# Where the softmax's normalisation is done: from a scaled identity on TensorE to a multiply on GpSimd, with the score scale moved into the exponential

## The chip, the cores and the metric

The kernel runs on one NeuronCore of a Trainium2 chip. The metric is the device time of one execution in microseconds (us). Engines are named as in the profile: PE is TensorE's matmul (PEld its weight load), DVE is VectorE, ACT ScalarE, POOL (Pool) GpSimd, SP SyncE.

## The reference

One encoder block over 512 tokens of width 2048, in fp32. A normed and modulated input is projected once; the projection feeds two groups of eight attention heads. Then come an output projection and an MLP. What matters here is the attention, where all heads look at all 512 tokens:

```
def block(i):                                   # group A: 8 query heads, 2 key heads, width 128
    s = einsum("bkgqd,bksd->bkgqs", qb, k) * (1 / sqrt(128))
    p = softmax(s, axis=-1)
    return einsum("bkgqs,bksd->bkgqd", p, v)

def block(i):                                   # group B: 8 heads, own keys, plus a shared rotary key of 64
    s = (einsum("bhqd,bhsd->bhqs", qn, k_nope)
         + einsum("bhqr,bsr->bhqs", qp, k_pe)) * (1 / sqrt(192))
    p = softmax(s, axis=-1)
    return einsum("bhqs,bhsd->bhqd", p, v)

o = concatenate([rms_norm(o_a, g_out_a), rms_norm(o_b, g_out_b)])     # over each group's 1024 columns
```

The rms_norm of the attention's outputs needs, for each token, the sum of squares over the heads of its group.

## The kernel before

Every matmul operand is split in a high and a low part of type fp32r, so that a product is three matmuls (high x high, high x low, low x high). ACT makes the high part, a copy rounded to fp32r, and DVE the low part, the difference (names ending in _hi and _lo). fp32 matmuls without that split are used only where the operand must not be rounded, as in the turning of the probabilities.

The stages follow each other: projection (blocks of 512 columns), latent keys and values, attention, output projection, MLP. Each engine runs its own program in order; semaphores tie them together. In the attention stage, the 16 heads run one after the other: head H is 0 to 7 for group A and 8 to 15 for group B. The tokens that ask are cut in four blocks t of 128.

For head H and block t:
- PE, `scores`: three matmuls of 512 columns (six in group B, where the rotary part is added) into bank[t].
- DVE, `row_max`: the negated maximum of each row into `top`. The queries had been multiplied by 1/sqrt(128) or 1/sqrt(192) when ACT copied them out of PSUM (`copy_out`, `turned_copy`).
- ACT, `exp`: prob = exp(score + top), with the row sums in `total` (a second record, the read of the accumulator).
- DVE, `invert`: the reciprocal of the sum, then scale_p = identity x reciprocal (128x128).
- PE, `turn_probs` (a "turn"): four fp32 matmuls, stationary operand a 128x128 piece of prob and moving operand scale_p. They transpose the piece and normalise it in one go. Blocks 0 and 3 share bank 4, so turn 3 waits until turned_lo(0) has read it.
- ACT, `turned_hi`, and DVE, `turned_lo`: the high and low part of the turned probabilities (pt_hi, pt_lo).
- PE, `attend`: when all four low parts are there, the product with the values, twelve matmuls into bank 6 (lines 1918 to 1920).
- ACT, `head_out` and `head_squares`: copy the product of head H-1 out, and square it into sq. Pool, `add_squares`, adds sq to sq_sum. head_squares(H) waits until Pool has added the square before it, since sq is one buffer.

The heads overlap by a written order. While head H's probabilities are turned, the scores of head H+1 are made: PE runs turn 0, turn 1, scores 0, turn 2, scores 1, turn 3, scores 2, scores 3, product. DVE runs turned_lo(0), row_max(0), turned_lo(1), turned_lo(2), row_max(1), invert(0), turned_lo(3), row_max(2), invert(1), row_max(3), invert(2), the low part of the next query (q_lo), invert(3); row_max and invert are head H+1's. ACT runs turned_hi(0), turned_hi(1), head_squares, turned_hi(2), exp(0), turned_hi(3), exp(1), exp(2), the high part of the next query, exp(3). head_out stands ahead of turned_hi(0) in group A. In group B there come besides: on ACT the high part of the values (v_hi) at the head's start, and after exp(3) those of the rotary query (qr_hi) and the key (k_hi); on DVE their low parts v_lo, at the head's start, and qr_lo and k_lo, at its end. The next head's scores 0 wait for k_lo. The next query's high part waits for all scores of the head before it.

Pool does nothing else in this stage. Ahead of it, it sets sq_sum to zero; behind it, it issues the loads of the residual once the sums of squares have been reduced. In the first head, DVE also has a part of the gate's modulation to do (`modulate_out`, tile ga_acc), between q_lo and the first turned_lo.

Of the kernel before, what the change touches and what calls it, by code (L numbers as in the profile page):

```python
# [26 lines left out]
P = 128  # L27
T = 512
NT = T // P
# [6 lines left out]
HEADS = 8  # L36
# [111 lines left out]
def build(nc, a, out, x1_dram, y_dram):  # L148
    with ExitStack() as ctx:
# [36 lines left out]
        rstd = small("rstd", [NT, 4])  # L186
        top = small("top", [NT])
        total = small("total", [NT])
        rtotal = small("rtotal", [NT])
# [11 lines left out]
        prob = sb("prob", 52, [NT, T])  # L201
        scale_p = sb("scale_p", 178, [NT, P])
        kg_hi, kg_lo = sb("kg_hi", 60, [2, T], F32R), sb("kg_lo", 64, [2, T], F32R)
# [110 lines left out]

        s_done, nb_ready, exp_done, rt_ready = sems("s_done nb_ready exp_done rt_ready")
        p_turned, pt_hi_done, pt_done, pv_done, o_done = sems("p_turned pt_hi_done pt_done pv_done o_done")
# [309 lines left out]
        def _(act):  # L626
# [61 lines left out]
            def copy_out(b):  # L688

                s = sets[b % 2]  # L690
                if b == 0:
                    for t in range(NT):
                        nc.scalar.activation(tok[:, t, :], s[t][:], ACT.Square, accum_out=stat[:, t, 0:1]).then_inc(c_sq, 1)
                elif b == 1:
                    for t in range(NT):
                        nc.scalar.activation(tok[:, t, 0:2 * P], s[t][:, 0:2 * P], ACT.Copy)
                        nc.scalar.activation(v_gqa[:, t, :, :].rearrange("p g e -> p (g e)"), s[t][:, 2 * P:4 * P], ACT.Copy).then_inc(copied, 1)
                elif b <= 4:
                    for t in range(NT):
                        nc.scalar.activation(tok[:, t, :], s[t][:], ACT.Copy).then_inc(copied, 1)  # L700
                elif b <= 6:
                    for n in range(4):
                        nc.scalar.activation(q_o[:, HEADS + 4 * (b - 5) + n, :], s[n][:], ACT.Copy, scale=SCALE_B).then_inc(copied, 1)
                elif b <= 8:
                    for n in range(4):
                        nc.scalar.activation(k_nope[:, 4 * (b - 7) + n, :], s[n][:], ACT.Copy).then_inc(copied, 1)
                else:
                    for t in range(NT):
                        dst = v_lat[:, t, 4 * (b - 9):4 * (b - 9) + 4, :].rearrange("p h e -> p (h e)")
                        nc.scalar.activation(dst, s[t][:], ACT.Copy).then_inc(copied, 1)  # L710

            def turned_copy(b):

                for n in range(TURNS[b]):
                    act.wait_ge(turned, TURNS_SUM[b] + n + 1)
                    src = sets[b % 2][n][:]
                    if b == 0:
                        k = 3 * KD + 2 * HEADS + n
                        nc.scalar.activation(ckv[:, n, :], src, ACT.Copy, scale=gains[:, k:k + 1]).then_inc(turned_out, 1)
                    elif b == 1:  # L720
                        nc.scalar.activation(k_gqa[:, n, :], src, ACT.Copy).then_inc(turned_out, 1)
                    elif b <= 3:
                        nc.scalar.activation(q_o[:, 4 * (b - 2) + n, :], src, ACT.Copy, scale=SCALE_A).then_inc(turned_out, 1)
                    else:
                        nc.scalar.activation(q_rot[:, n, :], src, ACT.Copy, scale=SCALE_B).then_inc(turned_out, 1)

# [86 lines left out]

            def exp(t, H):
                act.wait_ge(nb_ready, H * 4 + (t + 1))
                nc.scalar.activation(prob[:, t, :], bank[t][:], ACT.Exp, bias=top[:, t:t + 1], accum_out=total[:, t:t + 1]).then_inc(exp_done, 1)

# [13 lines left out]
            def attend(cur, nxt, after, first=False):  # L831
# [15 lines left out]
                if nxt:  # L847
                    exp(0, nxt[2])
                turned_hi(3, H)
                if nxt:  # L850
                    exp(1, nxt[2])
                    exp(2, nxt[2])
                if after:
                    stage_q(*after)
                if nxt:
                    exp(NT - 1, nxt[2])
                if after and after[0]:
# [4 lines left out]
            for t in range(NT):  # L862
                exp(t, 0)
            stage_q(*A(1))
# [189 lines left out]
        def _(dve):  # L1054
# [280 lines left out]

            def row_max(t, H):

                dve.wait_ge(s_done, H * 4 + (t + 1))
                nc.vector.reduce_max(top[:, t:t + 1], bank[t][:], AX.X, negate=True).then_inc(nb_ready, 1)

            def invert(t, H):

                dve.wait_ge(exp_done, H * 4 + (t + 1))
                own.step(nc.vector.reciprocal(rtotal[:, t:t + 1], total[:, t:t + 1]))
                ts(scale_p[:, t, :], ident[:], rtotal[:, t:t + 1], None, ALU.mult).then_inc(rt_ready, 1)

# [5 lines left out]
            def attend(cur, nxt, after):  # L1352
# [4 lines left out]
                if nxt:  # L1357
                    row_max(0, nxt[2])
                turned_lo(1, H)
                turned_lo(2, H)  # L1360
                if nxt:
                    row_max(1, nxt[2])
                    invert(0, nxt[2])
                turned_lo(3, H)
                if nxt:
                    for t in (2, 3):
                        row_max(t, nxt[2])
                        invert(t - 1, nxt[2])
# [12 lines left out]
            for t in range(NT):  # L1381
                row_max(t, 0)
                if t:
                    invert(t - 1, 0)
# [335 lines left out]
        def _(pe):  # L1720
# [170 lines left out]
            def turn_probs(t, H):  # L1891
                pe.wait_ge(rt_ready, H * 4 + (t + 1))

                behind = {0: 0, 1: -2, 2: -1, 3: 1}[t]
                if not isinstance(H, int):
                    pe.wait_ge(pt_done, H * 4 + behind)
                elif H * 4 + behind > 0:
                    pe.wait_ge(pt_done, H * 4 + behind)
                for c in range(NT):
                    ins = mm(bank[TURN_BANK[t]][:, c * P:(c + 1) * P], prob[:, t, c * P:(c + 1) * P], scale_p[:, t, :], start=True, stop=True)  # L1900
                ins.then_inc(p_turned, 1)
# [203 lines left out]
        def _(pool):  # L2105
# [8 lines left out]
            own.step(nc.gpsimd.memset(kr_lo[0:64, 1, :].bitcast(F32), 0.0))  # L2114

            def add_squares(H, grp):

                pool.wait_ge(o_done, H + 1)
                if not (isinstance(H, int) and H == 0):
                    pool.wait_ge(sq_ready, H)  # L2120
                tt(sq_sum[:, grp, :], sq_sum[:, grp, :], sq[:], ALU.add).then_inc(sq_ready, 1)

            pool.wait_ge(mod_reduced, NB + 3)
            own.step(nc.gpsimd.memset(sq_sum[:], 0.0))
            add_squares(0, 0)
            with pool.Fori(1, HEADS) as h:
                add_squares(h, 0)
            with pool.Fori(HEADS, 2 * HEADS - 1) as h:
                add_squares(h, 1)

# [80 lines left out]
```

## Time and profile before

| | |
|---|---|
| median of 3 runs | 2241.33 us (2238.19 to 2241.94) |
| profiled execution, its own time | 2241.33 us |
| its span, first to last instruction | 2239.7 us |
| busy: PE, DVE, ACT, POOL | 94%, 66%, 37%, 3% |
| mean granted TensorE clock | 0.978 of full |
| attention stage in the span | about 510 to 687 us |

A line of instructions has the start in us from the span's start, the duration in us, the engine, the line of the kernel, the operation, the tile written, the tiles read, and their shapes; "x16" says that sixteen records in a row were put together, and in square brackets stands how long the engine had been idle before it and who ended that. A fp32 matmul leaves two records, other matmuls one. PE's ends are modelled.

### The profile page before, as it was taken

The numbers are of one execution on the slowest core, as the hardware profiler recorded it, in microseconds if no ns is written. First come the engines' busy times: TensorE is split into PE (matmuls) and PEld (weight loads), VectorE is DVE, ScalarE is ACT, GpSimd is POOL, SyncE is SP. The second block draws the span as 40 slices with busy tenths as digits, with TensorE's granted clock in tenths as the row PEclk, the third lists the DMA queues.
The fourth block names the chain that finished last, engine by engine and source line by source line (L and its number), as shares of the span: only waits on it lengthen the run. The fifth ranks groups of instructions, "written<-read, shape, count | busy, mean of one in ns | idle before, by whom it ended". The sixth has DMA issues, their size and how long they took to land.

```text
span 2239.7 us, 27119 instructions
## 1 busy us (share of the span) xinstructions
PE 2115.9 (94%) x9652; PEld 1757.2 (78%) x9652; DVE 1477.7 (66%) x1754; ACT 821.4 (37%) x1103; POOL 74.9 (3%) x85
## 2 busy tenths in 40 slices
PE   2479999998999998999999999999999999999998
PEld 2368888887888887888888888888878888888886
DVE  5755687468775666554454455444688888889866
ACT  3233322246774235332332233233333333333322
POOL 0000000001110000000000000002100000000000
PEclk9679999999999999999999999999999999999999
DMA  8865666681004653476566556656774564456451
GB/s 298 292 227 175 205 169 194 191 259 57 1 0 157 212 194 137 143 247 215 179 211 232 184 184 231 212 179 235 292 275 152 221 233 175 172 225 257 157 186 76
DMA packets 199609, 427.76 MB, mean 191 GB/s; under 512 B 29908, under 2 KB 55160, under 8 KB 190712
## 3 DMA queue, kind: packets, MB, share of 16 engines
q1 hardware_dynamic: 180824, 349.89, 47.0%
q0 software_dynamic: 16704, 67.11, 8.4%
q10 hardware_dynamic: 2016, 9.90, 1.1%
q8 instruction: 40, 0.66, 0.1%
q14 instruction: 25, 0.20, 0.0%
HBM read 359.75 MB, written 67.11 MB: 191 GB/s over the span
## 4 chain that ended last, share of the span: by engine, by line
PE 85%; DVE 6%; DMA 4%; issue 2%; ACT 2%; SPq 0%; DVEq 0%; ACTq 0%; POOLq 0%
PE bank L1742 12%; PE bank L1743 12%; PE bank L1744 12%; PE bank L2035 6%; PE bank L2037 6%; PE bank L2036 6%; PE bank L1730 6%; PE bank L1731 6%; PE bank L1732 6%; DMA raw<-in_w_ada 2%; PE bank L1900 2%; DVE start_acc L1114 1%; PE bank L2082 1%; PE bank L2083 1%; PE bank L2084 1%
## 5 line engine op out<-in xcount | busy, mean ns | idle before, releaser
L1062 DVE TENSOR_TENSOR lo<-raw,hi 128x1024 fp32r<-128x1024 f32 x232 | 278.1, 1203 | 474.0 <-ACT hi L633 473.6
L633 ACT ACTIVATE hi<-raw 128x1024 fp32r<-128x1024 f32 x232 | 239.6, 1038 | 741.3 <-PE bank L1744 482.9
L1742 PE MATMUL bank<-h_hi,hi 128*128 128x512 f32 x1152 | 449.7, 390 | 3.5 <-DVE h_lo L1493 3.5
L1744 PE MATMUL bank<-h_hi,lo 128*128 128x512 f32 x1152 | 448.8, 390 | 0.0
L1743 PE MATMUL bank<-h_lo,hi 128*128 128x512 f32 x1152 | 448.7, 390 | 0.0
L2035 PE MATMUL bank<-hi,y_use 128*128 128x512 f32 x784 | 306.5, 391 | 7.7 <-DVE acc L1637 3.8
L2037 PE MATMUL bank<-hi,y_use 128*128 128x512 f32 x784 | 305.1, 389 | 0.0
L2036 PE MATMUL bank<-lo,y_use 128*128 128x512 f32 x784 | 305.1, 389 | 0.0
L1005 ACT ACTIVATE hi<-w 128x1024 fp32r<-128x1024 f32 x168 | 178.4, 1062 | 294.8 <-PE bank L2037 217.6
L1742 PEld LDWEIGHTS bank<-h_hi,hi 128*128 128x128 f32 x1152 | 216.6, 188 | 48.8 <-DVE h_lo L1493 3.7
L1743 PEld LDWEIGHTS bank<-h_lo,hi 128*128 128x128 f32 x1152 | 216.7, 188 | 45.1 <-issue 0.2
L1744 PEld LDWEIGHTS bank<-h_hi,lo 128*128 128x128 f32 x1152 | 216.6, 188 | 45.1
L1561 DVE TENSOR_TENSOR lo<-w,hi 128x1024 fp32r<-128x1024 f32 x168 | 204.4, 1221 | 40.8 <-ACT hi L1005 39.4
L2035 PEld LDWEIGHTS bank<-hi,y_use 128*128 128x128 f32 x784 | 147.1, 188 | 44.1 <-issue 13.9
L2037 PEld LDWEIGHTS bank<-hi,y_use 128*128 128x128 f32 x784 | 147.1, 188 | 30.7
L2036 PEld LDWEIGHTS bank<-lo,y_use 128*128 128x128 f32 x784 | 147.2, 188 | 30.1
L1730 PE MATMUL bank<-hi,h_hi 128*128 128x512 f32 x320 | 128.6, 402 | 0.7 <-issue 0.7
L1731 PE MATMUL bank<-lo,h_hi 128*128 128x512 f32 x320 | 127.0, 397 | 0.0
L1732 PE MATMUL bank<-hi,h_lo 128*128 128x512 f32 x320 | 126.6, 396 | 0.0
L1637 DVE TENSOR_TENSOR acc<-bank,acc 128x1024 f32<-128x1024 f32 x84 | 102.3, 1218 | 0.0
L1730 PE MATMUL bank<-hi,o_hi 128*128 128x512 f32 x224 | 89.2, 398 | 0.4 <-issue 0.4
L1114 DVE SCALAR_TENSOR_TENSOR start_acc<-raw,silu_c,start_acc 128x1024 f32<-128x1024 f32 x56 | 71.0, 1281 | 25.5 <-DMA raw<-in_w_ada 25.4
(274 smaller groups left out, 2871.0 us busy)
## 6 DMA issues: line engine op xcount, KB each, us to landing
raw<-in_w_ada SPq DMA_DIRECT2D x192, 512.0 KB, 4.7
raw<-in_w_mlp_in SPq DMA_DIRECT2D x128, 512.0 KB, 3.9
w<-in_w_mlp_out SPq DMA_DIRECT2D x128, 512.0 KB, 5.3
y_dram<-y_out POOLq DMA_DIRECT2D x32, 1792.0 KB, 8.3
y_use<-y_dram SPq DMA_DIRECT2D x53, 1024.0 KB, 8.8
raw<-in_w_in SPq DMA_DIRECT2D x32, 512.0 KB, 4.4
raw<-in_w_out SPq DMA_DIRECT2D x32, 512.0 KB, 4.6
raw<-in_w_in SPq DMA_DIRECT2D x48, 256.0 KB, 3.4
```

What stands on the lines that cost most here:

```text
L633: ins = nc.scalar.activation(dst, src, ACT.Copy)
L1062: ins = tt(dst, src, high.bitcast(F32), ALU.subtract)
L1561: tt(lo[w.slot()][:], weight(np, i, h)[:], hi[w.slot()][:].bitcast(F32), ALU.subtract).then_inc(dn_lo, 1)
L1730: mm(acc[t][:], xh, hi[s][:, q, :], start=first and q == 0, stop=False)
L1731: mm(acc[t][:], xh, lo[s][:, q, :], start=False, stop=False)
L1732: ins = mm(acc[t][:], xl, hi[s][:, q, :], start=False, stop=last and q == QROWS - 1)
L1742: mm(acc[n][:], wh, act_hi[:, k, :], start=first and q == 0, stop=False)
L1743: mm(acc[n][:], wh, act_lo[:, k, :], start=False, stop=False)
L1744: ins = mm(acc[n][:], wl, act_hi[:, k, :], start=False, stop=last and q == QROWS - 1)
L2035: mm(bank[b + m][:], yh, hi[s][:, q, :], start=j == 0, stop=False)
L2036: mm(bank[b + m][:], yh, lo[s][:, q, :], start=False, stop=False)
L2037: ins = mm(bank[b + m][:], yl, hi[s][:, q, :], start=False, stop=j == PAIRS - 1)
```

## The change

The normalisation goes from PE to Pool. scale_p and its build fall away; `invert` only makes the reciprocal. A new function on Pool, `normalise`, multiplies prob in place by the reciprocal of its row, one 128x512 multiply for each block, and a new semaphore p_ready lets PE turn the block, now by a transpose with the plain identity. On Pool the order becomes normalise(0), normalise(1), and then, for each following head, normalise(h+1) and add_squares(h-1); the last add follows the loop.

The score scale goes from the queries' copies into `exp`. The queries stay unscaled; row_max makes the plain maximum, and a second DVE instruction multiplies it by minus the scale into nbias.

```
-                        nc.scalar.activation(q_o[:, HEADS + 4 * (b - 5) + n, :], s[n][:], ACT.Copy, scale=SCALE_B).then_inc(copied, 1)
+                        nc.scalar.activation(q_o[:, HEADS + 4 * (b - 5) + n, :], s[n][:], ACT.Copy).then_inc(copied, 1)
...
-            def exp(t, H):
+            def exp(grp, t, H):
                 act.wait_ge(nb_ready, H * 4 + (t + 1))
-                nc.scalar.activation(prob[:, t, :], bank[t][:], ACT.Exp, bias=top[:, t:t + 1], accum_out=total[:, t:t + 1]).then_inc(exp_done, 1)
+                nc.scalar.activation(prob[:, t, :], bank[t][:], ACT.Exp, bias=nbias[:, t:t + 1],
+                                     scale=SCALE_B if grp else SCALE_A, accum_out=total[:, t:t + 1]).then_inc(exp_done, 1)
...
-            def row_max(t, H):
-
+            def row_max(grp, t, H):
                 dve.wait_ge(s_done, H * 4 + (t + 1))
-                nc.vector.reduce_max(top[:, t:t + 1], bank[t][:], AX.X, negate=True).then_inc(nb_ready, 1)
+                own.step(nc.vector.reduce_max(top[:, t:t + 1], bank[t][:], AX.X))
+                ts(nbias[:, t:t + 1], top[:, t:t + 1], -(SCALE_B if grp else SCALE_A), None, ALU.mult).then_inc(nb_ready, 1)
 
             def invert(t, H):
-
                 dve.wait_ge(exp_done, H * 4 + (t + 1))
-                own.step(nc.vector.reciprocal(rtotal[:, t:t + 1], total[:, t:t + 1]))
-                ts(scale_p[:, t, :], ident[:], rtotal[:, t:t + 1], None, ALU.mult).then_inc(rt_ready, 1)
+                nc.vector.reciprocal(rtotal[:, t:t + 1], total[:, t:t + 1]).then_inc(rt_ready, 1)
...
             def turn_probs(t, H):
-                pe.wait_ge(rt_ready, H * 4 + (t + 1))
+                pe.wait_ge(p_ready, H * 4 + (t + 1))
...
-                    ins = mm(bank[TURN_BANK[t]][:, c * P:(c + 1) * P], prob[:, t, c * P:(c + 1) * P], scale_p[:, t, :], start=True, stop=True)
+                    ins = nc.tensor.transpose(bank[TURN_BANK[t]][:, c * P:(c + 1) * P], prob[:, t, c * P:(c + 1) * P], ident[:])
                 ins.then_inc(p_turned, 1)
...
+            def normalise(H):
+
+                for t in range(NT):
+                    pool.wait_ge(rt_ready, H * 4 + (t + 1))
+                    tt(prob[:, t, :], prob[:, t, :], rtotal[:, t:t + 1].broadcast_to([P, T]), ALU.mult).then_inc(p_ready, 1)
+
             def add_squares(H, grp):
 
                 pool.wait_ge(o_done, H + 1)
-                if not (isinstance(H, int) and H == 0):
-                    pool.wait_ge(sq_ready, H)
+                pool.wait_ge(sq_ready, H)
                 tt(sq_sum[:, grp, :], sq_sum[:, grp, :], sq[:], ALU.add).then_inc(sq_ready, 1)
...
-            add_squares(0, 0)
-            with pool.Fori(1, HEADS) as h:
-                add_squares(h, 0)
-            with pool.Fori(HEADS, 2 * HEADS - 1) as h:
-                add_squares(h, 1)
+            normalise(0)
+            normalise(1)
+            with pool.Fori(1, HEADS + 1) as h:
+                normalise(h + 1)
+                add_squares(h - 1, 0)
+            with pool.Fori(HEADS + 1, 2 * HEADS - 1) as h:
+                normalise(h + 1)
+                add_squares(h - 1, 1)
+            add_squares(2 * HEADS - 2, 1)
```

The copies in `turned_copy` lose their scale in the same way.

## Rows read from the trace of the kernel before

**Rows 1.** The page: its first line, and the engines' shares of the last chain.
```profile
span 2239.7 us, 27119 instructions
...
PE 85%; DVE 6%; DMA 4%; issue 2%; ACT 2%; SPq 0%; DVEq 0%; ACTq 0%; POOLq 0%
```

**Rows 2.** Windows: stretch, length, busy PE, PEld, DVE, ACT, POOL, clock, DMA share, GB/s.
```profile
504.60:508.10 3.50, 3.50 (x9) 2.30 (x7) 3.39 (x5) 0.01 (x1) 0.22 (x1) 0.52 0.37 98
...
525.41:581.74 56.33, 56.08 (x337) 48.01 (x336) 43.92 (x104) 40.99 (x91) 7.72 (x6) 1.00 0.00 1
594.01:676.42 82.41, 82.41 (x477) 72.31 (x476) 64.96 (x139) 57.98 (x124) 9.02 (x7) 1.00 0.00 0
```

**Rows 3.** Timeline of PE: transposes, one-column matmuls, and turns.
```profile
40.78 8.65 PE L1759 MATMUL bank<-ident,x_tok 128*128 128x128 f32 x64 [34.70 <-DVE x_tok L1153]
...
221.83 1.91 PE L1810 MATMUL bank<-ident,tok 128*128 128x128 f32 x16
223.50 0.48 PE L1730 MATMUL bank<-hi,h_hi 128*128 128x512 f32 x1
...
500.11 3.63 PE L1861 MATMUL bank<-ones,mod_acc 128*128 128x1 f32 x32
...
562.96 1.95 PE L1900 MATMUL bank<-scale_p,prob 128*128 128x128 f32 x16
...
564.66 0.48 PE L1877 MATMUL bank<-kg_hi,q_hi 128*128 128x512 f32 x1
```

**Rows 4.** Timeline of one head of group A: the steps from its square on.
```profile
565.44 0.59 ACT L825 ACTIVATE sq<-bank 128x512 f32<-128x512 f32 x1
...
566.10 1.29 POOL L2121 TENSOR_TENSOR sq_sum<-sq_sum,sq 128x512 f32<-128x512 f32 x1 [8.10 <-ACT sq L825]
...
566.53 0.60 ACT L829 ACTIVATE pt_hi<-bank 128x512 fp32r<-128x512 f32 x1 [0.50 <-PE bank L1900]
...
567.16 0.69 DVE L1349 TENSOR_TENSOR pt_lo<-bank,pt_hi 128x512 fp32r<-128x512 f32 x1 [0.23 <-ACT pt_hi L829]
...
567.77 0.68 DVE L1339 TENSOR_REDUCE top<-bank 128x1 f32<-128x512 f32 x1
...
568.37 0.15 DVE L1344 RECIPROCAL rtotal<-total 128x1 f32<-128x1 f32 x1
...
568.76 0.68 DVE L1349 TENSOR_TENSOR pt_lo<-bank,pt_hi 128x512 fp32r<-128x512 f32 x1
```

**Rows 5.** Timeline of POOL and of DVE in the MLP; the page's row of the split.
```profile
L1062 DVE TENSOR_TENSOR lo<-raw,hi 128x1024 fp32r<-128x1024 f32 x232 | 278.1, 1203 | 474.0 <-ACT hi L633 473.6
...
1559.29 1.82 POOL L2167 TENSOR_TENSOR gm_acc<-gm_acc,rows 128x512 f32<-128x512 f32 x1 [4.75 <-DMA rows<-in_g_post_mlp]
1561.19 1.62 POOL L2168 TENSOR_TENSOR gm_acc<-gm_acc,rows 128x512 f32<-128x512 f32 x1
...
1568.92 1.29 POOL L2168 TENSOR_TENSOR gm_acc<-gm_acc,rows 128x512 f32<-128x512 f32 x1
...
1559.88 1.78 DVE L1524 TENSOR_TENSOR y_out<-y_mix,y_out 128x512 fp32r<-128x512 f32 x1
...
1569.02 2.28 DVE L1062 TENSOR_TENSOR lo<-raw,hi 128x1024 fp32r<-128x1024 f32 x1 [3.01 <-ACT hi L633]
```

**Rows 6.** Timeline of ACT: two turned_hi in a row, last head.
```profile
679.85 1.11 ACT L829 ACTIVATE pt_hi<-bank 128x512 fp32r<-128x512 f32 x2
```

**Rows 7.** Timeline of group B: first scores, row_max(3), k_lo, next first scores.
```profile
583.85 0.50 PE L1877 MATMUL bank<-k_hi,q_hi 128*128 128x512 f32 x1 [0.17 <-DVE k_lo L1272]
...
591.49 0.69 DVE L1339 TENSOR_REDUCE top<-bank 128x1 f32<-128x512 f32 x1 [0.30 <-PE bank L1888]
...
594.67 0.69 DVE L1272 TENSOR_TENSOR k_lo<-k_nope,k_hi 128x512 fp32r<-128x512 f32 x1
...
595.71 0.48 PE L1877 MATMUL bank<-k_hi,q_hi 128*128 128x512 f32 x1
```

**Rows 8.** Timeline of DVE in the first head.
```profile
515.17 3.11 DVE L1074 SCALAR_TENSOR_TENSOR ga_acc<-raw,silu_c,ga_acc 128x512 f32<-128x512 f32 x4
```

More of the change, by code:

```diff
@@ L187, in build @@
         top = small("top", [NT])
+        nbias = small("nbias", [NT])
         total = small("total", [NT])
@@ L201, in build @@
         prob = sb("prob", 52, [NT, T])
-        scale_p = sb("scale_p", 178, [NT, P])
         kg_hi, kg_lo = sb("kg_hi", 60, [2, T], F32R), sb("kg_lo", 64, [2, T], F32R)
@@ L312, in build @@
         q_hi_done, k_hi_done, qk_ready, v_hi_done, v_ready = sems("q_hi_done k_hi_done qk_ready v_hi_done v_ready")
-        s_done, nb_ready, exp_done, rt_ready = sems("s_done nb_ready exp_done rt_ready")
+        s_done, nb_ready, exp_done, rt_ready, p_ready = sems("s_done nb_ready exp_done rt_ready p_ready")
         p_turned, pt_hi_done, pt_done, pv_done, o_done = sems("p_turned pt_hi_done pt_done pv_done o_done")
@@ L722, in turned_copy @@
                     elif b <= 3:
-                        nc.scalar.activation(q_o[:, 4 * (b - 2) + n, :], src, ACT.Copy, scale=SCALE_A).then_inc(turned_out, 1)
+                        nc.scalar.activation(q_o[:, 4 * (b - 2) + n, :], src, ACT.Copy).then_inc(turned_out, 1)
                     else:
-                        nc.scalar.activation(q_rot[:, n, :], src, ACT.Copy, scale=SCALE_B).then_inc(turned_out, 1)
+                        nc.scalar.activation(q_rot[:, n, :], src, ACT.Copy).then_inc(turned_out, 1)
             roots = 0
@@ L847, in attend @@
                 if nxt:
-                    exp(0, nxt[2])
+                    exp(nxt[0], 0, nxt[2])
                 turned_hi(3, H)
                 if nxt:
-                    exp(1, nxt[2])
-                    exp(2, nxt[2])
+                    exp(nxt[0], 1, nxt[2])
+                    exp(nxt[0], 2, nxt[2])
                 if after:
@@ L855, in attend @@
                 if nxt:
-                    exp(NT - 1, nxt[2])
+                    exp(nxt[0], NT - 1, nxt[2])
                 if after and after[0]:
@@ L862, in _ @@
             for t in range(NT):
-                exp(t, 0)
+                exp(0, t, 0)
             stage_q(*A(1))
@@ L1357, in attend @@
                 if nxt:
-                    row_max(0, nxt[2])
+                    row_max(nxt[0], 0, nxt[2])
                 turned_lo(1, H)
@@ L1361, in attend @@
                 if nxt:
-                    row_max(1, nxt[2])
+                    row_max(nxt[0], 1, nxt[2])
                     invert(0, nxt[2])
@@ L1366, in attend @@
                     for t in (2, 3):
-                        row_max(t, nxt[2])
+                        row_max(nxt[0], t, nxt[2])
                         invert(t - 1, nxt[2])
@@ L1381, in _ @@
             for t in range(NT):
-                row_max(t, 0)
+                row_max(0, t, 0)
                 if t:
```

## The prediction

> **What bounds the kernel now.** I read the page first: the chain that ended last is 85% TensorE over a span of 2239.7 us [rows 1]. The change touches only the attention stage, some 510 to 687 us, so the busy times of its two groups came next [rows 2]. In group A (heads 1 to 6) PE is busy 56.08 of 56.33 us, in group B (heads 8 to 14) 82.41 of 82.41, by modelled ends; DVE has 78 and 79%, ACT 73 and 70%, Pool 14 and 11%. PE bounds both. A head takes 56.33 / 6 = 9.39 us in A and 82.41 / 7 = 11.77 in B. Hardly any DMA runs beside them (share 0.00), so what is saved or lost here moves everything behind by as much. The profiled execution's own time is 2241.33 us, also the median of the runs, so the sum is made against 2241.3.
>
> **PE: cheaper turns.** Sixteen fp32 matmuls a head turn the probabilities, each of two records: eight (x16) fill the 1.70 us from 562.96 to 564.66, so a block t of four fills 0.85. The transposes of the projection stage have one record each; 16 of them fill the 1.67 us from 221.83 to 223.50, a block so 0.42 [rows 3]. The change saves 4 x 0.43 = 1.7 us of PE a head, 27 us over 16 heads. That is the ceiling. What it gives depends on what ends last next, so I laid out one head of each group.
>
> **DVE and ACT.** The build of scale_p goes, four times a head; in return every row maximum is followed by a wait on itself and a 128x1 multiply. Start to start, a reciprocal with scale_p and the next operation lie 0.39 apart [rows 4]; without scale_p I take 0.09. The multiply is in no row; the nearest is the 128x1 reciprocal (0.15). I take 0.71 from maximum to multiply (0.68 and 0.03, the step from turned_hi's end to turned_lo) and 0.08 from there to the next operation (bounds 0 and 0.2). DVE's total hardly moves, but each exp starts some 0.17 later. ACT's work stays: the scales move out of copies into exp, inside instructions that run anyway; the read of the accumulator stays too.
>
> **Pool.** It gets four 128x512 multiplies a head, between the reciprocal and the turn, beside the add of squares: 5 x 1.29 = 6.45 us, by the add of that size [rows 4]. A broadcast column as operand is in no row; I bound the price by 0.69, DVE's for the size, and 1.82, Pool's slowest [rows 4, 5], and take 1.29, the same engine's. Pool's new order matters as much: the add for head H-2 now stands behind the four multiplies of head H, and ACT's head_squares(H) waits for it, with turned_hi(2) of that head queued behind, and DVE's turned_lo(2), row_max(1) and reciprocal(0) of the next head behind that. This closes a loop through Pool. Before, the add was finished 8 us before the next square.
>
> **Group A, from the end of one add to the end of the next**, start to start [rows 4, 6]: Pool to ACT 0.07 (as ACT's sq to Pool); sq 0.51; turned_hi(2) to turned_lo(2) 0.63; to row_max(1) 0.61; multiply 0.71; reciprocal(0) 0.08: together 2.61. Pool could begin the next head's first block at 2.83 (0.15 and 0.07 more). Its second waits for reciprocal(1), behind turned_lo(3) and row_max(2): 2.61 + 0.09 + 0.61 + 0.71 + 0.08 + 0.15 + 0.07 = 4.32. From there Pool is never idle: three multiplies and the add, 4 x 1.29 and 3 gaps of 0.08 [rows 5] = 5.40, end at 9.72. PE is no longer what sets the head: its work is at most 9.39 - 1.7 = 7.7. So A takes 9.7 instead of 9.39, a loss of 0.3 a head.
>
> **A shared port.** Pool and those DVE operations that have two SBUF inputs hold each other up here. At 1559.88 one of DVE took 1.78 us instead of 0.69; Pool's, begun before it, still had 1.23 to go. At 1569.02 a split took 2.28 instead of its mean 1.20 under a Pool multiply begun just before. And Pool's own at 1559.29 and 1561.19 took 0.53 and 0.33 too long [rows 5]. It looks like a lock held for an instruction, given next to who waits. The Trainium skill ("GPSIMD Engine Reference", the property table in section 1) names this contention, for DVE instructions with two SBUF inputs; the trace agrees, with +1.09 us at 1559.88. In A one such operation (q_lo, 0.69) falls between two Pool multiplies and holds Pool up by 0.4 (bounds 0 and 0.53). A head of A: 10.1, +0.7.
>
> **Group B.** PE alone would need 11.77 - 1.7 = 10.1. But the chain through k_lo is next [rows 7]: row_max(3) starts at 591.49, exp(3), qr_hi, k_hi, qr_lo and k_lo follow, and k_lo ends at 595.36, 3.87 later; the next scores came 0.35 after it, since PE was still turning. With two turns ahead of them shortened by 0.43 each, PE is there 0.5 too early. From a head's first scores (583.85) to row_max(3) are 7.64, less two turns 6.8. With a free port the period is 6.8 + 3.87 + 0.17 (multiply) + 0.06 = 10.9. Here q_lo, qr_lo, k_lo and v_lo all have two SBUF inputs, and Pool is busy 6.45 of some 12 us. In my layout qr_lo comes due 9.5 after the first scores, while Pool's block 2 runs; block 3 then slips in between qr_lo and k_lo and holds k_lo by one Pool instruction, some 1.2; v_lo, held up by the add, costs about 0.1 more. I take 12.2, +0.4 a head; bounds 10.9 (no collision) and 13.3 (two Pool instructions ahead of k_lo).
>
> **The edges.** First head: Pool's four multiplies take about 511.5 to 516.9, while DVE is to run q_lo and, from 515.17, four ga_acc updates of 0.78 with two SBUF inputs [rows 8]: +1.5 by one Pool instruction and a remainder, less 0.4 of a turn, +1.1 (bounds 0 and 2). Head 1, from its first turn to its product: two shorter turns ahead of DVE's chain and no add to wait for yet, -0.9. Into group B: two more multiplies of DVE ahead of k_lo (0.3) and one Pool instruction (1.2), +1.5. After the last first scores: two turns -0.85, and of the 1.7 of the last four turns a third, since ACT's copies fill the rest: together -1.4. Nothing changes behind the stage; Pool's loads of x_res follow the same semaphore.
>
> **Sum.** Start 1.1 - 0.9 = +0.2; five A periods, from the product of head 1 to that of head 6, x 0.7 = +3.5; into B +1.5; seven B periods x 0.4 = +2.8; end -1.4. Together +6.6: **2248 us**.
>
> **Rivals.** (a) Faster: the port costs nothing, because k_lo and Pool's blocks miss each other, or because a multiply by a column doesn't take the port. It decides at one place, the pair qr_lo and k_lo, if block 3 has ended before qr_lo comes due, some 1.5 us earlier than I have it. Then the start is -0.9 in all, A +0.3, B -0.9: -0.9 + 1.5 + 0.3 - 6.3 - 1.4 = -6.8, 2235. For it: DVE operations with a PSUM input beside Pool kept 0.69 (567.16 lies under Pool's add), so it is only four operations a head. Against: Pool is busy more than half of the time. (b) Everything is hidden and PE stays the bound: -27, 2214. Against it are the loop and the 3.87. (c) Slower: two Pool instructions ahead of k_lo in every second head (7 x 0.5 = +4) or a multiply dearer by 0.3 (5 instructions x 5 periods, +7.5): 2252 to 2256, middle 2255. (d) The clock. After 3.6 us of one-column matmuls it was granted at 0.52 (1.2 GHz nearly throughout) from 504.6 to 508.1 [rows 2, 3]. The new head leaves PE idle over 2.4 of 10.1 us in A, mostly in a piece ahead of the product. Were the whole stage at 1.2 GHz, PE's 7.7 and 10.1 us would double: heads of 15.4 and 20.2, (6.0 x 7 + 8.4 x 8) = some +110 at most, 2350. Both groups stood at 1.00 before, which speaks against it. The Trainium skill ("TensorE: Matmul & The Clock Gate", Part 4) says that transposes don't count as busy for this gate. By it only the other matmuls, 6.0 of 10.1 us, would hold the clock up, and the cost would be up to those 110 us. By the row it is nothing: 64 transposes alone ran for 8.65 us from 40.78, 0.135 each with their waits, not far from the 0.104 of the sixteen above [rows 3]. (e) Gains in B and losses in A cancel: 2241; it is (a) with half of the collisions.
>
> **How the numbers follow.** Under 0.2% (4.5 us) a measurement of this kernel can't be told from no change. Forecast, 2244 to 2252: 0.40; (a) 0.23; (b) 0.04; (c) 0.15; (d) 0.03; (e) 0.15. The range, 2231 to 2258, takes in (a), (c) and (e) with the bound of B's period without collision (7 x -1.3 = -9) and leaves out (b), (d) and the tails of (a) and (c), some 0.15. Forecast's own range: 2244 to 2252. Slower: most of the forecast (0.32), (c), (d): 0.50. Faster: (a), (b): 0.27. Same: (e) and the forecast's near end: 0.23.
>
> **What would show it.** The turns: 256 records instead of 512, a block in 0.42. Pool busy over half of the stage, multiplies at 1.29, more beside a q_lo, k_lo or v_lo. In A: ACT's sq waits for Pool's sq_sum, PE idles 2 us and more until turned_lo(3), period 10.1. In B: the first scores released by k_lo, k_lo or qr_lo well over 0.7, period near 12.2. I am wrong if those operations keep 0.69 beside Pool (B then 10.9), if Pool's multiply isn't near 1.29, or if the stage's clock leaves 1.00.

## The result, and the profile after

The changed kernel takes 2257.9 us (median of 4 runs, 2253.76 to 2261.32) against 2240.43 for the kernel before beside it: a ratio of 1.0078, 95% interval 1.0055 to 1.0100, 0.8% slower. The forecast was 2248, range 2231 to 2258, with slower as the likeliest outcome (0.50). The direction holds. The size does not: +17.5 us by the medians against +6.6 by the sum. The time lies within the range by 0.1 us, and not by the mechanism that the sum was made of. The profiled execution of the kernel after took 2253.06 us, 11.7 more than that of before; both traces are compared on those 11.7.

The page's lines that answer to [rows 1]:

```profile
span 2251.4 us, 26714 instructions
...
PE 83%; DVE 7%; DMA 4%; issue 3%; ACT 2%; POOL 1%; DVEq 0%; SPq 0%; ACTq 0%; POOLq 0%
```

Pool is now in the chain, and TensorE's share has fallen by two points. Group A first. One round of the loop through Pool, in the timeline of the kernel after (ACT, DVE, Pool and PE; lines between left out):

```profile
543.90 1.28 POOL L2125 TENSOR_TENSOR sq_sum<-sq_sum,sq 128x512 f32<-128x512 f32 x1
...
545.22 0.60 ACT L826 ACTIVATE sq<-bank 128x512 f32<-128x512 f32 x1 [1.12 <-POOL sq_sum L2125]
...
546.34 0.69 DVE L1348 TENSOR_TENSOR pt_lo<-bank,pt_hi 128x512 fp32r<-128x512 f32 x1 [0.58 <-ACT pt_hi L830]
...
547.66 0.15 DVE L1340 TENSOR_SCALAR nbias<-top 128x1 f32<-128x1 f32 x1
...
547.97 1.04 POOL L2119 TENSOR_TENSOR prob<-prob,rtotal 128x512 f32<-128x512 f32 x1 [2.78 <-DVE rtotal L1344]
...
548.53 0.50 PE L1917 MATMUL bank<-pt_hi,v_hi 128*128 128x512 f32 x1 [1.39 <-DVE pt_lo L1348]
...
549.41 3.70 POOL L2119 TENSOR_TENSOR prob<-prob,rtotal 128x512 f32<-128x512 f32 x3 [0.40 <-DVE rtotal L1344]
...
553.07 1.29 POOL L2125 TENSOR_TENSOR sq_sum<-sq_sum,sq 128x512 f32<-128x512 f32 x1
```

The loop is the one that was forecast. ACT's square waits for Pool's add, and from the add's end at 545.18 Pool's second block starts 4.23 later (forecast 4.32). But a multiply by a broadcast column takes 1.04 and not 1.29, and the next follows 1.00 after its start. From add to add a head takes 553.07 - 543.90 = 9.17 us. That is 0.22 *less* than before, where 10.1 was forecast.

Group B is another matter. In the timeline of the kernel after, one head's end and the next one's first scores:

```profile
631.53 2.56 POOL L2119 TENSOR_TENSOR prob<-prob,rtotal 128x512 f32<-128x512 f32 x2 [0.34 <-DVE rtotal L1344]
...
633.45 1.19 DVE L1272 TENSOR_TENSOR qr_lo<-q_rot,qr_hi 128x512 fp32r<-128x512 f32 x1 [1.06 <-ACT k_hi L774]
...
634.05 1.71 POOL L2125 TENSOR_TENSOR sq_sum<-sq_sum,sq 128x512 f32<-128x512 f32 x1
...
634.56 1.75 DVE L1273 TENSOR_TENSOR k_lo<-k_nope,k_hi 128x512 fp32r<-128x512 f32 x1
...
636.23 0.68 DVE L1335 TENSOR_TENSOR v_lo<-v_lat,v_hi 128x512 fp32r<-128x512 f32 x1
...
636.37 0.79 PE L1876 MATMUL bank<-k_hi,q_hi 128*128 128x512 f32 x1 [2.30 <-DVE k_lo L1273]
```

Read it as turns at one door. Pool's block 3 ends at 634.09; only then does qr_lo get on (1.19 instead of 0.69). Pool's add is held until qr_lo is done (1.71 instead of 1.29). Then k_lo is held until the add is done (1.75 instead of 0.69), and PE stands idle for 2.30 us. DVE's groups over the stage, kernel after, show that every head of B pays this (mean in ns; an unheld one of that size takes 685):

```profile
L1273 DVE TENSOR_TENSOR k_lo<-k_nope,k_hi 128x512 fp32r<-128x512 f32 x8 | 14.0, 1747 | 0.0
...
L1272 DVE TENSOR_TENSOR qr_lo<-q_rot,qr_hi 128x512 fp32r<-128x512 f32 x8 | 9.8, 1230 | 7.5 <-ACT k_hi L774 7.5
```

Then there is the duration of the first scores above: 0.79, against 0.50 in [rows 7]. The windows of the kernel after (columns as in [rows 2]):

```profile
595.40:599.00 3.60, 3.56 (x11) 2.87 (x12) 1.78 (x3) 0.07 (x1) 0.00 (x0) 0.53 0.02 5
622.20:626.10 3.90, 3.90 (x12) 3.18 (x13) 2.49 (x5) 0.55 (x3) 0.00 (x0) 0.57 0.00 0
626.10:636.40 10.30, 8.00 (x42) 6.44 (x40) 8.03 (x17) 7.79 (x18) 6.31 (x5) 1.00 0.00 0
636.40:640.10 3.70, 3.70 (x11) 2.98 (x12) 1.85 (x4) 0.03 (x1) 0.00 (x0) 0.54 0.00 0
640.10:650.50 10.40, 8.12 (x42) 6.58 (x40) 8.53 (x18) 8.25 (x18) 6.33 (x5) 1.00 0.00 0
```

TensorE's granted clock falls to its lower level (1.2 GHz), each time at the end of PE's wait for k_lo or up to 0.6 us behind it, and comes back. A mean of 0.53 over 3.60 us is some 3.4 us at half the clock, and the others come to the same. That happens in five of the eight heads of B (the other two windows lie behind 663.1 and 677.3). The periods between first scores show its price: 12.59 where the clock stays at 1.00, 14.18 where it falls, so 1.59 us a fall.

The profiled difference by the forecast's steps: from the stage's first scores to those of B +0.8 (forecast +5.2); seven B periods +11.8 (forecast +2.8), which is 7 periods longer by some 0.8 for the held operations, +5.4, and four falls of 1.59, +6.4; the end +0.4 with the fifth fall in it (forecast -1.4). Together +13.0 in the stage; the stage itself began 1.65 us earlier in that execution, and the rest differs by +0.3.

### The profile page after: what moved, and what is told of

Read it like the earlier page. It is cut to its first block, busy times and chain, and to the rows that moved or that the text cites. A ratio compares the mean times of both kernels' runs of the same rounds, so it can differ in the third digit from the quotient of the medians.

```text
span 2251.4 us, 26714 instructions
## 1 busy us (share of the span) xinstructions
PE 2100.6 (93%) x9396; PEld 1735.1 (77%) x9396; DVE 1484.4 (66%) x1754; ACT 819.6 (36%) x1103; POOL 151.0 (7%) x149
## 4 chain that ended last, share of the span: by engine, by line
PE 83%; DVE 7%; DMA 4%; issue 3%; ACT 2%; POOL 1%; DVEq 0%; SPq 0%; ACTq 0%; POOLq 0%
PE bank L1741 12%; PE bank L1743 12%; PE bank L1742 12%; PE bank L2034 7%; PE bank L2036 6%; PE bank L2035 6%; PE bank L1729 6%; PE bank L1731 6%; PE bank L1730 6%; DMA raw<-in_w_ada 2%; PE bank L2081 1%; PE bank L2083 1%; PE bank L2082 1%; DVE start_acc L1115 1%; PE bank L1787 1%
## 5 line engine op out<-in xcount | busy, mean ns | idle before, releaser
L1731 PE MATMUL bank<-hi,o_lo 128*128 128x512 f32 x224 | 87.2, 389 | 0.0
```

The lines of the kernel that those rows point to most:

```text
L1731: ins = mm(acc[t][:], xl, hi[s][:, q, :], start=False, stop=last and q == QROWS - 1)
```

## The experiments

Each ratio is to the kernel before, run on the same chip in the same session, with its 95% interval. "Stage" is the time from the first scores of head 0 to the first matmul of the output projection in the profiled execution: 184.6 us before, 197.6 after. "Period" is that of a head.

### Is the clock a cause of its own?

**after_again** is the changed kernel, unedited.

> The changed kernel once more, as the yardstick of the runs beside it: 2253 to 2261, 0.6 to 0.9% over the kernel before. Theory 1 (clock falls whose place is chance add 1.6 us each in group B): the number of heads of group B with their first scores at half clock is 3 to 7 and explains the time to 1 us. Rival (the clock has no part in it): the same number of falls, or none, at different times.

Measured: 2256.89 us, 1.0066 (1.0044 to 1.0089), stage 199.6. A 9.17; B 12.57 and 12.61 at full clock, 13.76 (the first) to 14.18 in the five periods with a fall. In the last head the clock was low for another 6.8 us, behind waits of 1.60 and 1.41 us, which the first trace doesn't have. That the falls explain the time to 1 us did not come true: the two profiled executions of this kernel (2253.06 and 2257.98) lie 4.9 us apart, and only 2.0 of that are in the stage.

**filler** gives PE something to do ahead of its wait for k_lo:

```
             def scores(grp, h, H, t):
                 if t == 0:
+                    if grp:
+                        for _ in range(6):
+                            mm(bank[0][:], kr_hi[:, 0, 0:P], kr_hi[:, 0, :], start=True, stop=True)
                     pe.wait_ge(qk_ready, H + 1)
```

> The changed kernel, and in group B six 128x512 matmuls into bank 0, whose result is overwritten, ahead of PE's wait for k_lo. Theory 1 (the idle time of 2.3 us at that wait lets the clock fall, each fall costs 1.6 us): granted clock 1.00 all through group B, every period 12.6, 8 us less than the changed kernel, some 2248. Rival A (transposes in place of matmuls let the clock fall, wherever PE waits): falls stay, periods of 14.2 stay. Rival B (PE's work bounds the head): each head 1.4 us longer, 2268.

Measured: 2248.02 us, 1.0030 (1.0017 to 1.0042), stage 189.8. In its timeline of PE the fillers cover part of the wait, and k_lo still ends it; its window over the rest of B stands at clock 1.00:

```profile
608.58 1.62 PE L1871 MATMUL bank<-kr_hi 128*128 128x512 f32 x6
611.15 0.50 PE L1879 MATMUL bank<-k_hi,q_hi 128*128 128x512 f32 x1 [0.96 <-DVE k_lo L1273]
```
```profile
605.00:690.00 85.00, 76.26 (x383) 61.63 (x383) 67.28 (x132) 55.71 (x119) 43.59 (x35) 1.00 0.00 0
```

The first B period is 12.48, the others 12.59 to 12.62. Work that computes nothing made the kernel 8.9 us faster, by the medians of the same session. So the falls are a cause of their own, and the period without them is the loop through k_lo.

**mm_turns** gives PE its old work back, as part of the kernel rather than as padding:

```
-                    ins = nc.tensor.transpose(bank[TURN_BANK[t]][:, c * P:(c + 1) * P], prob[:, t, c * P:(c + 1) * P], ident[:])
+                    ins = mm(bank[TURN_BANK[t]][:, c * P:(c + 1) * P], prob[:, t, c * P:(c + 1) * P], ident[:], start=True, stop=True)
```

> The changed kernel, but its turns of the probabilities are four-pass fp32 matmuls by the plain identity again in place of transposes, so PE gets back the work that the change took off it (about 1.7 us a head). Nothing else differs. Theory 1 (in the stage the loops that set the period don't go through PE's work: GpSimd's loop in the first part, the late k_lo in the second; and PE's wait of about 2.3 us for k_lo is what the granted clock falls after): the first part's period stays 9.17, the second's is 12.6 as in the changed kernel at full clock, PE's wait shrinks to 0.6 to 1.4 us, the clock stays at 1.00, and the time is 2246 to 2250, below the changed kernel's 2257. Rival (PE's work counts in each head, as it did in the kernel before): 1.7 us more a head, about 2280.

Measured: 2257.62 us, 1.0072 (1.0057 to 1.0088), stage 199.5. The clock part held: PE's wait is 1.26 to 1.41 us (2.09 at the first head), and there is no fall in group B.

```profile
629.61 0.50 PE L1876 MATMUL bank<-k_hi,q_hi 128*128 128x512 f32 x1 [1.38 <-DVE k_lo L1273]
```
```profile
605.00:690.00 85.00, 76.63 (x432) 65.98 (x432) 66.45 (x129) 53.25 (x114) 38.90 (x31) 1.00 0.00 0
```

The time was missed by 9 us: the period of A is 9.42 (the second block starts 4.47 after the add's end instead of 4.23, so a quarter of a microsecond of the turns is in that loop too), and the period of B is 13.48 and not 12.6. The chain of waits of the kernel after shows why. Columns: start, duration, what; between k_lo and row_max(3) two turns lie on it:

```profile
626.56 0.24 PE bank L1885
...
627.26 0.44 PE bank L1899 x4
...
630.50 0.70 DVE top L1339
```

The other of the two stands at 624.66, under the low clock. The loop through k_lo contains two turns a head, so dearer turns lengthen it by 2 x 0.44: 12.59 + 0.88 = 13.47. Both theories were wrong on the period. The change's cheaper turns do save 0.9 us a head in B, and the loss of the clock (five falls, 8.0 us) takes that back: the kernel is as slow with them as without (1.0066 of the kernel before with them, 1.0072 without).

### Which Pool instruction is in the way?

**early_add** moves Pool's add ahead of the multiplies of the next head:

```
-            with pool.Fori(1, HEADS + 1) as h:
-                normalise(h + 1)
+            add_squares(0, 0)
+            normalise(2)
+            with pool.Fori(2, HEADS + 1) as h:
                 add_squares(h - 1, 0)
-            with pool.Fori(HEADS + 1, 2 * HEADS - 1) as h:
                 normalise(h + 1)
+            with pool.Fori(HEADS + 1, 2 * HEADS - 1) as h:
                 add_squares(h - 1, 1)
+                normalise(h + 1)
```

> The changed kernel, with each add of squares on Pool ahead of the four multiplies that it followed. Theory 1 (a loop through Pool sets group A; in group B the add holds k_lo up at the shared port): a head of A falls from 9.17 to some 8.3 to 8.6, k_lo from 1.75 to 0.7 us, a head of B from 12.6 or 14.2 to 11.3 to 11.8 with no fall of the clock, the time to some 2234. Rival (the multiplies, not the add, hold up A and k_lo): A within 0.2 of 9.17, B within 0.3 of the changed kernel's.

Measured: 2238.49 us, 0.9979 (0.9969 to 0.9990), stage 180.4. A 8.50, B 11.52. The clock fell once in B's periods, behind a wait of 1.97 us, and once in the last head, behind the two waits of these lines, with one turn between them (timeline of PE):

```profile
676.23 0.63 PE L1899 MATMUL bank<-ident,prob 128*128 128x128 f32 x4 [0.83 <-DVE pt_lo L1348]
678.57 0.69 PE L1917 MATMUL bank<-pt_hi,v_hi 128*128 128x512 f32 x1 [1.71 <-DVE pt_lo L1348]
```

The steps came as theory 1 had them, the time 4 us above its 2234. In its timeline of DVE and of Pool, qr_lo still waits for block 3, but k_lo is free, and the add comes behind v_lo:

```profile
628.26 1.20 DVE L1272 TENSOR_TENSOR qr_lo<-q_rot,qr_hi 128x512 fp32r<-128x512 f32 x1 [1.06 <-ACT k_hi L774]
629.38 0.68 DVE L1273 TENSOR_TENSOR k_lo<-k_nope,k_hi 128x512 fp32r<-128x512 f32 x1
```
```profile
626.34 2.57 POOL L2119 TENSOR_TENSOR prob<-prob,rtotal 128x512 f32<-128x512 f32 x2 [0.32 <-DVE rtotal L1344]
630.86 1.29 POOL L2126 TENSOR_TENSOR sq_sum<-sq_sum,sq 128x512 f32<-128x512 f32 x1 [1.95 <-ACT sq L826]
```

The order of two instructions on an engine that is 7% busy over the whole span is worth 18 us, by the medians of that session (2256.89 to 2238.49): 0.67 a head in A, 1.07 a head in B, and most of the falls.

**pool_1col** and **pool_129** change what a multiply costs, and its operand (both leave the probabilities unnormalised, the first but for one column):

```
-                    tt(prob[:, t, :], prob[:, t, :], rtotal[:, t:t + 1].broadcast_to([P, T]), ALU.mult).then_inc(p_ready, 1)
+                    tt(prob[:, t, 0:1], prob[:, t, 0:1], rtotal[:, t:t + 1], ALU.mult).then_inc(p_ready, 1)
...
+                    cut = lambda x: x.rearrange("p (c n) -> p c n", c=NT)
+                    tt(cut(prob[:, t, :]), cut(prob[:, t, :]), ones[:].unsqueeze(1).broadcast_to([P, NT, P]), ALU.mult).then_inc(p_ready, 1)
```

> The changed kernel with Pool multiplying one column of each block instead of 512 (the probabilities stay unnormalised otherwise); order and waits stay. Theory 1: Pool's share of the port is what costs; qr_lo, k_lo and q_lo back at 0.69, A at 8.3 to 8.5, B at 10.9 to 11.2 without falls of the clock, some 2229. Rival (the order of waits costs, whatever Pool's work lasts): A stays within 0.3 of 9.17 and B over 12.

> The changed kernel with Pool multiplying by a block of ones (a real 128x512 operand, identity's size read four times) instead of the broadcast column; the probabilities stay unnormalised. Theory 1 (in group A a loop through Pool holds four multiplies and an add): the multiply takes 1.29 instead of 1.04 and a head of A 9.17 + 4 x 0.25 = 10.17, with the last turn and product waiting as before; group B 0 to 0.5 more a head. Rival (DVE's chain sets A): A moves by less than 0.3.

Measured: pool_1col 2235.08 us, 0.9968 (0.9953 to 0.9982), stage 176.3; A 8.49, B 11.32; k_lo 0.68, qr_lo 1.04 (the add is still ahead of it), no fall in B's periods and one in the last head, behind the same two waits. So the order of waits costs little once Pool's multiplies are short, against the rival. qr_lo, B and the time (by 6 us) came out above theory 1, which had left out that the add still holds qr_lo. pool_129 2268.53 us, 1.0133 (1.0117 to 1.0149), stage 205.9; its B periods are 13.07 at full clock, within the 0.5 that was expected, and 14.3 to 14.6 with a fall. Its multiplies, by Pool's timeline:

```profile
542.73 1.28 POOL L2120 TENSOR_TENSOR prob<-prob,ones 128x512 f32<-128x512 f32 x1 [2.78 <-DVE rtotal L1344]
544.17 4.25 POOL L2120 TENSOR_TENSOR prob<-prob,ones 128x512 f32<-128x512 f32 x3 [0.17 <-DVE rtotal L1344]
548.38 1.28 POOL L2126 TENSOR_TENSOR sq_sum<-sq_sum,sq 128x512 f32<-128x512 f32 x1
```

With a full second operand a multiply takes 1.28, the price I had taken. A's period became 9.71: +0.54, the growth of the three multiplies (4.25 against 3.70). The first isn't in the loop, since Pool waits there for the second reciprocal anyway; the expectation, 10.17, had counted four. It also takes my sum apart. At the full price the loop is 4.22 to the second block, 4.21 for three multiplies, 1.28 for the add. Of the 10.1 I had, 0.24 were gaps between Pool's instructions that don't exist and 0.10 a later start; the port's 0.4 is there, as 4.21 - 3 x 1.27.

### What is each part of the change worth?

**scale_exp** makes only the move of the scale, in the kernel before. **pool_a_only** moves only the normalisation, in group A only, with the early add. **early_qscale** is early_add with the scales back in the queries and the negated maximum in one instruction. One place of each (the first two against the kernel before, the third against the changed kernel):

```
+                own.step(nc.vector.reduce_max(top[:, t:t + 1], bank[t][:], AX.X))
+                ts(nbias[:, t:t + 1], top[:, t:t + 1], -(SCALE_B if grp else SCALE_A), None, ALU.mult).then_inc(nb_ready, 1)
...
+                pe.wait_ge(rt_ready if grp else p_ready, H * 4 + (t + 1))
...
-                nc.scalar.activation(prob[:, t, :], bank[t][:], ACT.Exp, bias=nbias[:, t:t + 1],
+                nc.scalar.activation(prob[:, t, :], bank[t][:], ACT.Exp, bias=top[:, t:t + 1], accum_out=total[:, t:t + 1]).then_inc(exp_done, 1)
```

> The kernel before with only the score scale moved into the exponential (plain maximum, wait, 128x1 multiply); scale_p and the fp32 turns stay. Theory 1 (the multiply lies 0.17 us ahead of each exp; in A two of them lie ahead of the product, in B PE has 0.35 us to spare): A 9.39 to some 9.7, B within 0.1 of 11.77, 1.5 to 2.5 us in all. Rival (it is a good part of the loss): B over 12.0, 5 us or more.

> The kernel before with the normalisation on Pool and transposes for the eight heads of group A alone, the adds of squares kept ahead of the multiplies, scales as before. Theory 1 (A gains when the add is not in its loop; B has nothing to gain with k_lo behind it): a head of A 8.2 to 8.4, B 11.77, no fall of the clock beyond those of before, -6 us, some 2236. Rival (switching groups costs what A gains): within 2 us of the kernel before.

> The changed kernel with the adds ahead of the multiplies (as early_add) and the scales back in the queries' copies, so no second DVE instruction behind the maximum. Theory 1 (each such instruction lies 0.17 on the chains that set both groups): A 8.50 to 8.2 to 8.35, B 11.4 to 11.5 to 11.2 to 11.3, 2 to 4 us less than early_add, some 2235. Rival (the DVE instruction is hidden): the same as early_add within 1 us.

| | median us | ratio | stage | A | B |
|---|---|---|---|---|---|
| scale_exp | 2243.51 | 1.0014 (1.0005 to 1.0023) | 187.4 | 9.57 to 9.60 | 11.80 to 11.91 |
| pool_a_only | 2232.75 | 0.9965 (0.9952 to 0.9977) | 176.6 | 8.09 | 11.77 |
| early_qscale | 2232.37 | 0.9962 (0.9949 to 0.9974) | 175.5 | 8.09 | 11.55 |

The move of the scale pays in neither kernel: it costs 2.8 us of stage by itself and 8.50 - 8.09 = 0.41 a head in A on top of the early add, more than the 0.15 to 0.3 that was expected. That this is because the extra multiply of DVE stands twice in the row of steps that A's period goes through is argued. In B beside the early add it is not seen (11.52 and 11.55), against theory 1 and for the rival; in scale_exp it is at most 0.14. The move of the normalisation pays in A, 1.3 us a head, once the add is out of the way.

### What bounds the best version?

Both kernels below bring the staging of the next key forward, on ACT ahead of exp(3) and on DVE ahead of invert(3):

```
-                if nxt:
-                    exp(NT - 1, nxt[2])
                 if after and after[0]:
                     stage_k(after[1])
+                if nxt:
+                    exp(NT - 1, nxt[2])
```

> The version with early adds and the scales kept in the queries, and in the second part the next head's key staging (qr_hi, k_hi on ScalarE, qr_lo, k_lo on VectorE) is issued ahead of the last exp and the last reciprocal of the head. Theory 1 (there the period of 11.55 is set by k_lo's place in the engines' orders, PE has about 1 us of idle a head): period 10.2 to 10.8, time 2224 to 2229. Rival (PE's own work, or the loop through the transposes, sets the period already): period 11.4 to 11.6, time 2231 to 2234.

> The kernel before with the same reorder of the key staging alone. Theory 1 (there PE's work sets the period of 11.77, and k_lo comes in time): no difference, within 2 us of the kernel before. Rival (k_lo's place sets the period there too, and the gain of the early version comes from the order alone): about 5 us less, 2235.

Measured: early_qscale_kfirst 2226.03 us, 0.9931 (0.9918 to 0.9944), stage 166.5, A 8.07, B 10.40. before_kfirst 2240.27 us, 0.9995 (0.9986 to 1.0005), B 11.77, no difference. So the order alone does nothing where PE is the bound, and 1.15 us a head where k_lo is. The window over seven heads of B in early_qscale_kfirst has PE busy for 71.91 of 72.70 us; TensorE is the bound again, as before the change, at a period shorter by 1.4:

```profile
578.70:651.40 72.70, 71.91 (x365) 58.82 (x365) 60.98 (x113) 56.66 (x127) 41.05 (x35) 1.00 0.00 0
```

This is the fastest version that was found, 15.5 us under the kernel before. Its exp(3) comes later than in the other kernels, without harm.

## Why the prediction came out so

- **Turns.** 0.44 a block (forecast 0.42), half of [rows 3]'s. Right. Neither group then had PE as its bound, as forecast.
- **DVE's steps.** Maximum to multiply 0.71, multiply to reciprocal 0.07, start to start: right (forecast 0.71 and 0.08). Add's end to reciprocal(0) 2.55 (2.61), to the second block 4.23 (4.32).
- **Pool's multiply** ("take 1.29, the same engine's") is the first mis-sized term: 1.04, within its bounds, and 1.00 from one start to the next instead of 1.37. q_lo held Pool by 0.6 instead of 0.4. A came out at 9.17 against 10.1, so five A periods gave -1.1 instead of +3.5. The row that I took it from, the add of [rows 4], has two full operands; pool_129, the same multiply with a second operand that is read in full, takes 1.28. Rival (c), at +7.5 for dearer multiplies, has a wrong sum besides: it counts five instructions a period, but only three multiplies lie in the loop, so 0.3 each would be 4.5.
- **The port.** The mechanism is as forecast. Of the four operations that were named, qr_lo and k_lo are held in every head of B, q_lo keeps its 0.69 and holds Pool up in A, and v_lo, forecast at +0.1, keeps 0.68 in all heads but the last. The Trainium skill ("SBUF — State Buffer", "SBUF: two separate sides") calls the shared port pair an exclusive lock that the first to start holds for its whole instruction. The trace agrees: k_lo's 1.75 ends 0.55 after Pool's add has ended, near the 0.69 that it takes alone.
- **B's period at full clock**, 12.59 against 12.2, is the second term. From first scores to row_max(3) it took 616.32 - 609.60 = 6.72 in a head at full clock, and 8.32 with the fall at 622.18 (forecast 6.8), right. From there to k_lo's end it took 636.31 - 630.50 = 5.81, where 3.87 + 0.17 + 1.2 = 5.24 was forecast. The step "block 3 then slips in between qr_lo and k_lo and holds k_lo by one Pool instruction" names the wrong instruction and too few: block 3 held qr_lo by 0.5, and the add slipped in and held k_lo by 1.06. early_add shows it by taking away the second and leaving the first.
- **The clock.** This is the step that failed. Rival (d) had the lower clock for the whole stage or not at all, put it in A, where PE waits longest in total, and gave it 0.03. It came in B, for 3.4 us at a time, after single waits of 2.2 to 2.3 us, and cost 6.4 us of the profiled B periods and 8.0 with the end; in A's periods there was none. My own layout left PE idle 12.2 - 10.1 = 2.1 us in B, and the chain through k_lo puts it at one place in each head. I laid the idle time out for A only. That a wait of 3.46 us can be enough stood in the trace of the kernel before, at the stage's first turn, where the clock is 0.50 from 511.40 to 514.80 (timeline of PE):

```profile
511.66 3.53 PE L1900 MATMUL bank<-scale_p,prob 128*128 128x128 f32 x16 [3.46 <-DVE scale_p L1345]
```

How much shorter such a wait may be, no row said. filler shows that filling this wait ends the falls.
- **Transposes and the clock.** The Trainium skill ("TensorE: Matmul & The Clock Gate", Part 4) says that transposes don't count as busy for the clock gate. The trace of the kernel before does not agree for fp32 transposes, and I read its row in [rows 3] too roughly. The mean of 0.135 is not transposes with waits, but two paces. Its timeline of PE in the windows 42:43 and 46:47 shows seven starts in a row 0.21 apart, then twelve 0.11 apart:

```profile
41.69 1.70 PE L1759 MATMUL bank<-ident,x_tok 128*128 128x128 f32 x7
45.75 1.47 PE L1759 MATMUL bank<-ident,x_tok 128*128 128x128 f32 x12
```

PE had been idle for 34.70 us ahead of them and ran nothing but transposes, and its pace doubled within them, as between its two levels of clock. In the trace of the kernel after, where this code is the same, the pace doubles 13 transposes later, so the step doesn't come from the program. (The windows give 1.00 for all of that stretch, even while PE was idle, so the spacing decides.) So fp32 transposes by themselves brought the clock up, and filler's B, whose turns are transposes, stood at 1.00 throughout. The whole-stage cost that I worked out beside that rule did not come. mm_turns shortened the wait and exchanged the transposes at once, so no run here holds the wait and exchanges them alone.
- **My own signs.** Two of the three that were to prove me wrong came: Pool's multiply isn't near 1.29, and the stage's clock left 1.00. PE's wait ahead of A's product is 1.4 to 1.5 us and not 2 and more.
- **Start and end.** First head +0.8 (forecast +1.1), ga_acc 3.88 instead of 3.11; in that head the clock was low for 6.8 us around PE's first wait, which was 4.73, where it had been 3.4 and 3.46 before; head 1 -0.9 as forecast; into B about +2.0 (+1.5); the end -1.2 without its fall (-1.4); filler's end, which has none, is 1.59 shorter than that of the kernel after.

The errors had both signs: the start and A came out 4.4 us below their terms, B 9.0 above, the end 1.8 above. The medians differ by 17.5 and the profiled executions by 11.7; that execution, at 2253.06, lies below all four timed runs, which spread over some 8 us. How many falls each of the other executions had is not seen. Their mean granted clock points that way (0.973 at 2253.76 and 2255.42, 0.971 and 0.972 at 2260.38 and 2261.32), but that the spread comes from the number of falls is argued, not shown.

Open: what decides whether a wait is followed by a fall. In the kernel after, waits of 2.19, 2.29, 2.30, 2.31 and 2.32 us were, and others of 2.31, 2.32 and 3.01 were not; one of 1.97 was in early_add, one of 2.09 was not in mm_turns. In pool_129 they are longer, 2.68 to 2.81 in seven heads, and no more of them were followed: four were, three were not. So the length of the wait alone doesn't decide. In the last head, where two waits lie close together (0.83 and 1.71), the clock fell in all four kernels that have this pair (early_add, pool_1col, early_qscale, early_qscale_kfirst); a single one of 1.69, in the kernel before and three others with fp32 matmuls as turns there, was never followed.

## What to carry to other kernels

Work moved to an idle engine brings that engine's order with it: lay out where each of its instructions falls beside those that share a port with it, and put the one that nobody waits for soon (here the add) where the late operations don't meet it. When the bounding engine is relieved, ask not only what bounds next, but how long in one piece TensorE will now stand still: here a wait of some 2.3 us cost another 1.6 in five of eight heads. And a price taken from "the same engine, the same size" needs the same operands too.

## What was not expected of the hardware

- Pool multiplies 128x512 fp32 by a broadcast column in 1.04 us, by a full operand in 1.28.
- TensorE's clock fell to its lower level for 3.4 us at a time after waits of 2.0 to 2.3 us, and after 0.83 and 1.71 close together, though PE was busy 83% of the time in group B; it did not fall after every such wait.
- A run of fp32 transposes alone, after 34.70 us of idle time, brought TensorE from a start every 0.21 us to one every 0.11.
- DVE and Pool took turns at the port: qr_lo, the add and k_lo each waited for the one before, at 1.19, 1.71 and 1.75 us instead of 0.69, 1.29 and 0.69.
